# First stage of a hybrid mixer layer: context squares summed on TensorE, odd context squares on VectorE, strip rows and modulation on ScalarE, three places for modulation weights

## The reference, cut to what matters

```python
def rmsnorm(x, g):
    y = x * lax.rsqrt(jnp.mean(x * x, axis=-1, keepdims=True) + EPS)
    return y * g

def adaln(cond, w_ada, b_ada):             # w_ada: 2048 x 6144
    mod = jax.nn.silu(cond) @ w_ada + b_ada
    shift, scale, gate = jnp.split(mod[:, None, :], 3, axis=-1)
    return shift, scale, gate

h_l = rmsnorm(x, norm_g) * (1.0 + sc) + sh          # 512 tokens
h_c = rmsnorm(ctx, norm_g) * (1.0 + sc_c) + sh_c    # 256 tokens
u_l = h_l @ w_in                                    # all columns
u_c = h_c @ w_in[:, OFF_KV:OFF_MLA_G]               # the key columns only
...                                                 # Hyena, attention, pooling
return rmsnorm(x + gt * (out @ w_out), final_norm_g)
```

## Time and profile before

| what | value |
|---|---|
| median of 3 runs | 1074.84 us (1074.23 to 1078.49) |
| the profiled execution, its own time | 1081.42 us |
| its span in the trace | 1079.6 us |
| granted TensorE clock, mean | 0.962 |
| PE busy | 970.1 us, 90% of the span |
| DVE busy | 585.6 us, 54% |
| ACT busy | 369.5 us, 34% |
| POOL busy | 87.5 us, 8% |
| moved by DMA | 136.15 MB, 126 GB/s over the span |

### The profile page before, as it was taken

The page is one execution under the profiler, slowest core; times in us unless marked ns, Lnnn a source line. Parts: engine busy times, 40 slices in busy tenths (PEclk is TensorE's granted clock), DMA queues, the critical chain, the costliest instruction groups (busy, mean ns, idle before and its releaser), DMA issues. The chain is left out here.

```text
span 1079.6 us, 12409 instructions
## 1 busy us (share of the span) xinstructions
PE 970.1 (90%) x5066; PEld 800.9 (74%) x5066; DVE 585.6 (54%) x818; ACT 369.5 (34%) x533; POOL 87.5 (8%) x77
## 2 busy tenths in 40 slices
PE   0799999899999999999999950889999969999996
PEld 0477777788787887888888830778898847888875
DVE  5444448657845677356632237477676665334144
ACT  6222245434325343122212232345454433123133
POOL 0122210300003000000000054000000000011010
PEclk9899999999999999999989985999999988999999
DMA  9789943212322112378833211110000027222313
GB/s 372 305 328 347 347 156 93 78 46 93 98 69 78 59 59 78 107 261 291 281 112 98 79 33 52 46 49 32 19 1 1 1 94 296 84 112 81 115 39 156
DMA packets 27252, 136.15 MB, mean 126 GB/s; under 512 B 3419, under 2 KB 3867, under 8 KB 19772
## 3 DMA queue, kind: packets, MB, share of 16 engines
q1 hardware_dynamic: 26764, 135.23, 35.4%
q10 hardware_dynamic: 432, 0.13, 0.1%
HBM read 131.16 MB, written 4.19 MB: 125 GB/s over the span
## 5 line engine op out<-in xcount | busy, mean ns | idle before, releaser
L850 PE MATMUL pp<-h_hi,w_hi 128*128 128x512 f32 x544 | 216.0, 397 | 7.9 <-DVE w_lo L584 4.7
L850 PE MATMUL pp<-h_lo,w_hi 128*128 128x512 f32 x544 | 213.8, 393 | 0.0
L850 PE MATMUL pp<-h_hi,w_lo 128*128 128x512 f32 x544 | 213.7, 393 | 0.0
L584 DVE TENSOR_TENSOR w_lo<-w_raw,w_hi 128x1024 fp32r<-128x1024 f32 x68 | 84.8, 1247 | 150.0 <-ACT w_hi L347 149.7
L347 ACT ACTIVATE w_hi<-w_raw 128x1024 fp32r<-128x1024 f32 x68 | 71.7, 1057 | 171.0 <-PE pp L850 143.8
L850 PEld LDWEIGHTS pp<-h_hi,w_hi 128*128 128x128 f32 x544 | 103.7, 191 | 32.4 <-DVE w_lo L584 5.5
L850 PEld LDWEIGHTS pp<-h_hi,w_lo 128*128 128x128 f32 x544 | 103.4, 190 | 22.0
L850 PEld LDWEIGHTS pp<-h_lo,w_hi 128*128 128x128 f32 x544 | 103.8, 191 | 20.8
L1797 PE MATMUL po<-wo_hi,m_hi 128*128 128x512 f32 x256 | 101.0, 395 | 6.5 <-DVE wo_lo L1728 6.5
L1797 PE MATMUL po<-wo_lo,m_hi 128*128 128x512 f32 x256 | 100.6, 393 | 0.0
L1797 PE MATMUL po<-wo_hi,m_lo 128*128 128x512 f32 x256 | 100.5, 393 | 0.0
(11 more groups left out here) (283 smaller groups left out, 1857.9 us busy)
## 6 DMA issues: line engine op xcount, KB each, us to landing
w_raw<-in_wb_dram SPq DMA_DIRECT2D x68, 512.0 KB, 3.6
ada_raw<-in_w_ada_dram SPq DMA_DIRECT2D x16, 2048.0 KB, 9.8
w_gate_raw<-in_w_gate_dram SPq DMA_DIRECT2D x16, 1024.0 KB, 4.9
wo_raw<-in_w_out_dram SPq DMA_DIRECT2D x16, 1024.0 KB, 4.8
wa_raw<-in_wa_dram SPq DMA_DIRECT2D x16, 320.0 KB, 4.0
UG<-in_xT_dram SPq DMA_DIRECT2D x4, 1024.0 KB, 10.1
y<-in_x_dram SPq DMA_DIRECT2D x4, 1024.0 KB, 12.1
out_dram<-y SPq DMA_DIRECT2D x8, 512.0 KB, 3.1
```

The costliest lines, as they stand in the source:

```text
L584: eng.tensor_tensor(lane(w_lo, n % KW), lane(raw, n % KW), lane(w_hi, n % 2), ALU.subtract).then_inc(wb_lo_done, 1)
L850: mm = eng.matmul(ps[i][:], w, x, start=(kk == 0 and m == 0), stop=(kk == KT - 1 and m == 2))
```

## The change

- The context squares no longer pass through VectorE's running sum. TensorE multiplies each of them by the matrix of ones as it comes, accumulating 16 matmuls in ps[6]; only x still goes through the sum in `rstd`, and one matmul (into ps[5]) totals it.
- The context squares of odd k are made by VectorE (a product of c_tile with itself), those of even k by ScalarE as before.
- `rows_out` and `modulation` run on ScalarE instead of VectorE. The added 1 of the scale column moves from the first instruction into the last, which is now g * m1 + g.
- On VectorE `scale(j)` and `tokens(j)` follow each other for every j, with nothing between them.
- w_ada has three places instead of two. The third lies where the next weights (w_hi, w_raw) come later, so the SP queue waits for ada_mm 15 before it loads these.
- On TensorE combine(2) and ada_vectors(2) move from before the first tile into step 0, behind its tile 1; combine(3) moves to the end of step 0.

```diff
@@ -86,7 +86,7 @@
         c_in_place, tmp, rstd = at("c_raw", TAB, KT * LC), at("h_tmp", TAB + 8, 2 * LK), at("rstd", TAB + 11, LK)
-        ada = at("ada_raw", 16, 2 * 4096)
+        ada = [at(f"ada_raw{s}", p, 4096) for s, p in enumerate((16, 24, FREE + 32))]
         wa_raw_ = at("wa_raw", 32, 2 * AW)
@@ -110,9 +110,6 @@
             return c_in_place[:, bass.ts(k, LC)]
-
-        def ada_ring(s):
-            return ada[:, s * 4096:(s + 1) * 4096]
 
@@ -165,13 +162,15 @@
         par_in, cond_in, const = sem("par_in"), sem("cond_in"), sem("const")
-        ada_in = [sem(f"ada_in{s}") for s in range(2)]
+        ada_in = [sem(f"ada_in{s}") for s in range(3)]
         wa_in = [sem(f"wa_in{s}") for s in range(2)]
...
         gate_in = [sem(f"gate_in{s}") for s in range(2)]
-        silu_done, spread_done = sem("silu_done"), sem("silu_spread_done")
+        silu_done = sem("silu_done")
         sq_done, sum_done = sem("sq_done"), sem("sum_done")
-        total_done, root_done, rstd_done = sem("total_done"), sem("root_done"), sem("rstd_done")
+        csq = [sem(f"ctx_sq{s}") for s in range(2)]
+        csum_mm = sem("ctx_sum_mm")
+        root_done = sem("root_done")
         ada_mm, rows_done, comb_mm = sem("ada_mm"), sem("rows_done"), sem("comb_mm")
@@ -212,13 +211,24 @@
 
-            for j in range(KT):
-                if j >= 2:
-                    eng.wait_ge(ada_mm, j - 1)
-                eng.dma_start(ada_ring(j % 2), t["w_ada"][j, :, :]).then_inc(ada_in[j % 2], 16)
+            def load_ada(j):
+                if j >= 3:
+                    eng.wait_ge(ada_mm, j - 2)
+                eng.dma_start(ada[j % 3][:], t["w_ada"][j, :, :]).then_inc(ada_in[j % 3], 16)
+
+            def load_wa(j):
                 if j >= 2:
...
                 eng.dma_start(wa_raw(j % 2), t["wa"][j, :, :]).then_inc(wa_in[j % 2], 16)
+
+            load_ada(0)
+            for j in range(KT):
+                if j == 1:
+                    load_wa(1)
+                if j + 1 < KT:
+                    load_ada(j + 1)
+                if j != 1:
+                    load_wa(j)
 
@@ -231,6 +241,7 @@
 
+            eng.wait_ge(ada_mm, KT - 1)
             for n in range(KW):
@@ -309,6 +320,20 @@
 
+            def rows_out(j):
+                eng.wait_ge(ada_mm, j + 1)
+                eng.activation(rows[:], ps[7][:, 0:256], ACT.Copy).then_inc(rows_done, 1)
+
+            def modulation(j):
+
+                m, m1 = mod[:, 4 * j:4 * j + 4], mod1[:, 2 * j:2 * j + 2]
+                g = par[:, P_NG + j:P_NG + j + 1]
+                eng.wait_ge(comb_mm, j + 1)
+                eng.activation(m1, ps[7][:, 258:260], ACT.Identity, bias=par[:, P_BSC + j:P_BSC + j + 1], scale=1.0).then_inc(mod_step, 1)
+                eng.activation(m[:, 0:2], ps[7][:, 256:258], ACT.Identity, bias=par[:, P_BSH + j:P_BSH + j + 1], scale=1.0).then_inc(mod_done, 1)
+                eng.wait_ge(mod_step, j + 1)
+                eng.activation(m[:, 2:4], m1, ACT.Identity, bias=g, scale=g).then_inc(mod_scale, 1)
+
             def rows_of_w(j):
@@ -320,25 +345,40 @@
             eng.activation(spread[:].rearrange("p (k r) -> p k r", r=32)[:, :, 0:2],
-                           silu_c[:].rearrange("p (k r) -> p k r", r=2), ACT.Copy).then_inc(spread_done, 1)
+                           silu_c[:].rearrange("p (k r) -> p k r", r=2), ACT.Copy).then_inc(silu_done, 1)
 
...
                 s = k % 2
-                eng.activation(tmp[:, s * LK:s * LK + L], x_tile(k), ACT.Square)
-                eng.activation(tmp[:, s * LK + L:(s + 1) * LK], c_tile(k), ACT.Square).then_inc(sq_done, 1)
-            eng.wait_ge(total_done, 1)
+                eng.activation(tmp[:, s * LK:s * LK + L], x_tile(k), ACT.Square).then_inc(sq_done, 1)
+                if k % 2 == 0:
+                    if k >= 2:
+                        eng.wait_ge(csum_mm, k - 1)
+                    eng.activation(tmp[:, s * LK + L:(s + 1) * LK], c_tile(k), ACT.Square).then_inc(csq[0], 1)
             eng.wait_ge(sum_done, KT)
+            eng.wait_ge(csum_mm, KT + 1)
             eng.activation(tmp[:, 0:L], ps[5][:], ACT.Sqrt, bias=eps[:, 0:1], scale=1.0 / D)
             eng.activation(tmp[:, L:LK], ps[6][:, 0:LC], ACT.Sqrt, bias=eps[:, 0:1], scale=1.0 / D).then_inc(root_done, 1)
+            eng.wait_ge(par_in, 48)
+            rows_out(0)
+            modulation(0)
             rows_of_w(0)
+            tokens(0)
+            rows_out(1)
+            modulation(1)
             rows_of_w(1)
+            rows_out(2)
             for j in range(KT):
-                tokens(j)
                 if 1 <= j < KT - 1:
                     rows_of_w(j + 1)
+                if j + 1 < KT:
+                    tokens(j + 1)
+                if j + 2 < KT:
+                    modulation(j + 2)
+                if j + 3 < KT:
+                    rows_out(j + 3)
 
@@ -517,18 +557,6 @@
 
-            def rows_out(j):
-                eng.wait_ge(ada_mm, j + 1)
-                eng.tensor_copy(rows[:], ps[7][:, 0:256]).then_inc(rows_done, 1)
-
-            def modulation(j):
-                m, m1 = mod[:, 4 * j:4 * j + 4], mod1[:, 2 * j:2 * j + 2]
-                eng.wait_ge(comb_mm, j + 1)
-                eng.tensor_scalar(m1, ps[7][:, 258:260], par[:, P_BSC + j:P_BSC + j + 1], 1.0, ALU.add, ALU.add).then_inc(mod_step, 1)
-                eng.tensor_scalar(m[:, 0:2], ps[7][:, 256:258], par[:, P_BSH + j:P_BSH + j + 1], None, ALU.add).then_inc(mod_done, 1)
-                eng.wait_ge(mod_step, j + 1)
-                eng.tensor_scalar(m[:, 2:4], m1, par[:, P_NG + j:P_NG + j + 1], None, ALU.mult).then_inc(mod_scale, 1)
-
             def scale(j):
@@ -551,33 +579,24 @@
             for k in range(KT):
+                s = k % 2
+                if s:
+                    eng.wait_ge(x_in[k // 4], 32)
+                    if k >= 2:
+                        eng.wait_ge(csum_mm, k - 1)
+                    eng.tensor_tensor(tmp[:, s * LK + L:(s + 1) * LK], c_tile(k), c_tile(k), ALU.mult).then_inc(csq[1], 1)
                 eng.wait_ge(sq_done, k + 1)
-                s = k % 2
                 if k == 0:
-                    eng.tensor_copy(rstd[:], tmp[:, 0:LK]).then_inc(sum_done, 1)
+                    eng.tensor_copy(rstd[:, 0:L], tmp[:, 0:L]).then_inc(sum_done, 1)
                 else:
                     eng.wait_ge(sum_done, k)
-                    eng.tensor_tensor(rstd[:], rstd[:], tmp[:, s * LK:(s + 1) * LK], ALU.add).then_inc(sum_done, 1)
-            eng.wait_ge(par_in, 48)
-            rows_out(0)
-            modulation(0)
+                    eng.tensor_tensor(rstd[:, 0:L], rstd[:, 0:L], tmp[:, s * LK:s * LK + L], ALU.add).then_inc(sum_done, 1)
             eng.wait_ge(root_done, 1)
-            eng.reciprocal(rstd[:], tmp[:, 0:LK]).then_inc(rstd_done, 1)
-            rows_out(1)
-            modulation(1)
-            eng.wait_ge(rstd_done, 1)
-            scale(0)
-            rows_out(2)
-            tokens(0)
+            eng.reciprocal(rstd[:], tmp[:, 0:LK]).then_inc(sum_done, 1)
+            eng.wait_ge(sum_done, KT + 1)
             for j in range(KT):
-                if j + 1 < KT:
-                    scale(j + 1)
-                if j + 1 < KT:
-                    tokens(j + 1)
-                if j + 2 < KT:
-                    modulation(j + 2)
-                if j + 3 < KT:
-                    rows_out(j + 3)
+                scale(j)
+                tokens(j)
 
@@ -797,8 +816,8 @@
                     eng.wait_ge(mod_step, j)
-                eng.wait_ge(ada_in[j % 2], 16 * (j // 2) + 16)
-                vectors(ada_ring(j % 2), ada_mm)
+                eng.wait_ge(ada_in[j % 3], 16 * (j // 3) + 16)
+                vectors(ada[j % 3][:], ada_mm)
 
@@ -818,24 +837,28 @@
 
-            eng.wait_ge(spread_done, 1)
+            eng.wait_ge(silu_done, 2)
             eng.wait_ge(const, 1)
+            for k in range(KT):
+                eng.wait_ge(csq[k % 2], k // 2 + 1)
+                s = k % 2
+                eng.matmul(ps[6][:, 0:LC], ones[:], tmp[:, s * LK + L:(s + 1) * LK], start=(k == 0), stop=(k == KT - 1)).then_inc(csum_mm, 1)
             eng.wait_ge(sum_done, KT)
-            eng.matmul(ps[5][:], ones[:], rstd[:, 0:L], start=True, stop=True)
-            eng.matmul(ps[6][:, 0:LC], ones[:], rstd[:, L:LK], start=True, stop=True).then_inc(total_done, 1)
+            eng.matmul(ps[5][:], ones[:], rstd[:, 0:L], start=True, stop=True).then_inc(csum_mm, 1)
             ada_vectors(0)
...
             ada_vectors(1)
-            combine(2)
-            ada_vectors(2)
             eng.wait_ge(root_done, 1)
...
                     mm = tile(i, j)
-                    if i == 1 and j + 2 < KT:
+                    if j == 0 and i == 1:
+                        combine(2)
+                        ada_vectors(2)
+                    if i == (1 if j else 4) and j + 2 < KT:
                         combine(j + 3)
```

## The result

| | before | after |
|---|---|---|
| median of 10 runs each | 1078.42 us (1074.23 to 1083.03) | 1071.86 us (1070.15 to 1074.63) |
| ratio, 95% interval | | 0.9945 (0.9924 to 0.9966) |
| the profiled execution, its own time | 1081.42 us | 1070.15 us |
| its span | 1079.6 us | 1068.4 us |
| granted TensorE clock, mean | 0.962 | 0.967 |

The kernel became faster by 0.55%, with an interval that reaches from 0.34% to 0.76%; the forecast was 0.34% faster, 1071.2 us. The three runs of before that stood ahead of the prediction are among its ten and lie low (their median is 1074.84), so that the time came out so near (1071.2 against 1071.86) is in part luck: the gain was forecast at 3.6 us and measured at 5.9 (0.0055 x 1078.42, 3.7 to 8.2).

The account below looks back on a forecast made before the run. TensorE, busy without waits from 60 to 130 us, was taken as the bound, so gains lie before the first tile: 10.0 us earlier start, 3.6 kept after step 0; 1074.84 - 3.6 = 1071.2 us, range 1067.5 to 1075.0.

Parts of the forecast that it names:

- Sum: VectorE's running sum of squares at the start: ends at 23.9 us instead of 26.06, bounds 23.3 to 24.7.
- Total: The one total left on TensorE after the sum: costs 0.9 us, at most 1.84, ending at 24.9.
- Table load: ScalarE's load before the roots: waits for the last total, so its 1.28 us stands on the path.
- Reciprocal: VectorE, directly behind the roots with nothing ahead of it: 27.3 to 32.25 us; 3.7 of the gain.
- The clock: TensorE idles from about 31.5 to 35.9 before the first tile; first 4.4 us afterwards expected at half speed.
- Step 0: First projection step: grows from 7.0 to 13.4 us through slow tiles, combines, waits and ada vectors; 3.6 gained remains.
- the stops: TensorE's waits for ScalarE's modulation columns ahead of ada vectors in step 0: 0.5 us each, at most 1.0.
- Steps of 7.04: Projection steps after the first stay at 7.04 us, with TensorE never waiting.
- the rival of ScalarE's pace: Late strip rows on ScalarE stop TensorE in each of 13 steps; 6.8 us net loss, 1081.6 us; chance 0.04.
- The third place: Third buffer place for w_ada: changes nothing, as there was no wait for a transfer to remove.
- The median: Whole kernel: profiled time 1081.42 less 3.6 gives 1077.8 us; median 1074.84 less 3.6 gives 1071.2 us.
- the later start: Rival at the kernel's start: clock, table load or ScalarE waits cost more; gain 1 to 2.5, 1073.1 us; chance 0.17.

Follow-up runs that it names:

- e1_table: Changed kernel with the two waits ahead of the roots exchanged, so the table load waits for VectorE's sum, not the last total; 1072.53 us, ratio 0.9953 to before.
- c_after: The changed kernel itself, unaltered, timed and traced a second time; 1071.04 us, ratio 0.9924 to the kernel before.
- e3_two_places: Changed kernel with two places for w_ada and the load order of the kernel before; 1074.57 us, ratio 0.9975 to the kernel before.
- e8_wa_first: e1_table with wa[0] loaded ahead of w_ada[1]; one run, 1068.17 us.
- e4_sums_only: Kernel before with only the new sums: context squares totalled on TensorE, odd ones made by VectorE; 1075.32 us, ratio 0.9964 to before.

## Why the prediction was right

The mechanism held: a start about 10 us earlier, about half of it lost again in a longer step 0 (forecast 6.4 lost of 10, measured 4.9 of 9.45), steps of 7.04 behind it. The nearness of the time is in part luck, as said above. Point by point, forecast and first execution of the changed kernel:

- **Sum** ends 23.9, measured 24.11 (23.43 + 0.68). The last context piece landed half a us later than taken (the square that waits for it starts at 20.09, forecast 19.6), and a pair of adds with its square took 1.73 instead of 1.8 (VectorE from 21.36 to 23.09).
- **Total** 0.9, measured 1.05 from start to the next start, against 1.84 before: the clock was at its upper level, as taken, and the ada vectors behind it took 1.93 where they took 2.83.
- **Table load** on the path, 1.28: it was. But had it been hidden, GpSimd would have held scale(0) (e1_table). I had named wa[0] as covered unless it was later than 33.5, and its low part was ready at 32.97. What I left out is that GpSimd, while it makes this low part, slows VectorE's scale(0); in the changed kernel the two overlap by only 0.2 (32.74 to 32.97), and scale(0) took 0.78.
- **Reciprocal** behind the roots, 27.3 to 32.25: 27.76 to 32.71. Start 35.9: 36.50. The gain at the start, 10.0, was 9.45.
- **The clock** fell in the gap ahead of the first tile, where I had it fall, and in this execution once before: in the gap ahead of ada_vectors(1) (0.83 over 28 to 30), which then took 3.30 and ended at 33.22, not at 31.5. It cost nothing at the start, since TensorE still waited 3.27 for the low part.
- **Step 0**, 13.4: 11.85 in the first execution (36.50 to 46.49 + 1.86), 13.8 in c_after. Of its terms the two slow tiles were right (2.8, 2.69 measured); combine(2) took 0.7 for 1.0, the stops 0.50 and 0.51 as said. The term mis-sized is ada_vectors(2), 2.8 forecast, 1.87 in one execution and 3.6 in the other: the clock comes back at 39.5 or at 44. A single number was not to be had for it; both ends stood in its bounds. That the forecast gain at step 1 (3.6) lies between those of the two executions (4.6 and 2.7, against the first of before) is therefore no merit of the 2.8.
- **Steps of 7.04**: right, the rival of ScalarE's pace did not come.
- **The third place** was the step that failed: "The third place therefore changes nothing." The slip was in the prediction ("about 2 us", measured 2.1), but the slack was taken as "two to three steps", which is what three places give, and the verdict was read off the trace of before, where TensorE waits for no transfer. With two places the slipped load has 9.05 us to land and takes 8.0 to 10.1, and 2.8 us come back (e3_two_places). It did no harm to the sum, because the change contains both the slip and its cure.
- **The median**: the profiled pair gave 11.2 us, the stage 4.6. Taking the difference of two spans for the change would have been wrong by a factor of two; the time forecast came nearer than the gain forecast because the runs shown of before lay low.
- **A rival's price**: for the later start the prediction says "gain 1 to 2.5"; its terms one at a time (0.9, 1.4, 1.0 off 3.6) give 2.2 to 2.7. It did not come.

## What to carry to other kernels

Before an engine's idle queue is called a cover, ask what the same edit does to it: an instruction moved behind a new wait shifts every load that hangs on it, and the slack has to be read in the changed order. When work is hidden by a long instruction, look also at what else runs at the moment it ends; two engines off the path can hold each other up and put one of them on it. Compare two traces at a landmark just behind the edit, and take a second trace of each kernel before a difference further on is explained.

## What the runs showed of the hardware

- VectorE with two SBUF inputs is held up while GpSimd's two-input instruction runs: 1.92 for 0.75 (e1_table), and 0.75 again when GpSimd is done before (e8_wa_first). An instruction on two columns took 1.23 for 0.22 and ended with GpSimd's, once (e4_sums_only). In the changed kernel the low parts (L575) take 1010 ns on average where they took 770, off the path.

```profile
L575 DVE SCALAR_TENSOR_TENSOR h_lo<-h_tmp,mod,h_hi 128x512 fp32r<-128x512 f32 x16 | 16.2, 1010 | 62.2 <-ACT hc_hi L320 62.2
```

- The granted clock fell in the changed kernel when TensorE had had a combine at 28.1 to 28.7 between two gaps of about 1 us (0.83 over 28 to 30, 0.50 over 30 to 32).
- One and the same program scatters by up to 1.9 us in its first 154 us (147.9 and 149.8, mostly by the moment at which the clock comes back: ada_vectors(2) 1.93 and 3.64), and by 6.8 us behind it (the kernel before, 920.3 to 927.1).
